# One fused fp32 network on one core: who takes the closing product, when the first weight pieces are split, and where the windowed attention's output is rounded

## The reference, cut to what matters

```python
for layer in range(DEPTH):                       # DEPTH = 2
    h = rms_norm(x, mix_pre_g[layer])
    m = pool_mixer(h, ...) if layer == 0 else swa_sink_attention(q, kk, vv, sinks) @ w_o
    x = x + rms_norm(m, mix_post_g[layer])
    f = conv_glu_ffn(rms_norm(x, ffn_pre_g[layer]), ...)   # 1024 -> 2 x 2816 -> 1024
    x = x + rms_norm(f, ffn_post_g[layer])
```

## Time and profile before

| | |
|---|---|
| median of 3 runs | 1634.32 us (1633.74 to 1635.6) |
| the profiled execution | 1632.63 us, span 1630.9 us |
| TensorE (PE) busy | 1588.7 us, 97% of the span |
| VectorE (DVE) busy | 1015.9 us, 62% |
| ScalarE (ACT) busy | 706.1 us, 43% |
| GpSimd (POOL) busy | 172.3 us, 11% |
| mean granted TensorE clock | 0.991 |

### The profile page before, as it was taken

The page is one execution under the profiler, slowest core; times in us unless marked ns, Lnnn a source line. Parts: engine busy times, 40 slices in busy tenths (PEclk is TensorE's granted clock), DMA queues, the critical chain, the costliest instruction groups (busy, mean ns, idle before and its releaser), DMA issues.

```text
span 1630.9 us, 21359 instructions
## 1 busy us (share of the span) xinstructions
PE 1588.7 (97%) x8046; PEld 1289.0 (79%) x8046; DVE 1015.9 (62%) x1894; ACT 706.1 (43%) x1391; POOL 172.3 (11%) x148
## 2 busy tenths in 40 slices
PE   7999999999998999999999999999999999999997
PEld 6888888888875788888888887766665888888887
DVE  6876666545768577666663376666666555554367
ACT  6544444333457545444442343344444443443252
POOL 0121111000002202111110000000011001110000
PEclk9999999999999999999999999999999999999998
DMA  6133333333120213333322424211110222222231
GB/s 223 55 108 96 97 99 101 105 110 104 46 75 27 75 52 102 96 92 99 102 97 96 139 97 119 64 47 46 40 39 27 97 91 97 97 98 97 97 110 65
DMA packets 91151, 143.69 MB, mean 88 GB/s; under 512 B 8740, under 2 KB 30756, under 8 KB 90920
## 3 DMA queue, kind: packets, MB, share of 16 engines
q1 hardware_dynamic: 88560, 136.58, 26.9%
q10 hardware_dynamic: 2488, 5.75, 1.1%
HBM read 140.19 MB, written 2.10 MB: 87 GB/s over the span
## 4 chain that ended last, share of the span: by engine, by line
PE 93%; DVE 2%; issue 2%; ACT 1%; DMA 1%; SPq 0%; POOL 0%; DVEq 0%; POOLq 0%; ACTq 0%
PE ps L433 23%; PE ps L434 23%; PE ps L435 23%; PE ps L1918 2%; PE ps L1920 2%; PE ps L1919 2%; PE ps L474 2%; PE ps L475 2%; PE ps L476 2%; PE ps L1599 1%; PE ps L1622 1%; PE ps L1642 1%; PE ps L1293 1%; PE ps L1322 1%; PE ps L1242 1%
## 5 line engine op out<-in xcount | busy, mean ns | idle before, releaser
L418 DVE TENSOR_TENSOR wl<-raw,wh 128x512 fp32r<-128x512 f32 (+2 forms) x425 | 307.4, 727 | 406.0 <-ACT wh L409 405.7
L409 ACT ACTIVATE wh<-raw 128x512 fp32r<-128x512 f32 (+2 forms) x425 | 264.6, 627 | 544.3 <-PE ps L435 541.3
L433 PE MATMUL ps<-Hh,wh 128*128 128x512 f32 x1148 | 452.4, 394 | 1.9 <-DVE Hl L1486 1.9
L435 PE MATMUL ps<-Hh,wl 128*128 128x512 f32 x1148 | 448.3, 390 | 0.0
L434 PE MATMUL ps<-Hl,wh 128*128 128x512 f32 x1148 | 448.2, 390 | 0.0
L433 PEld LDWEIGHTS ps<-Hh,wh 128*128 128x128 f32 x1148 | 216.1, 188 | 49.8 <-issue 2.4
L435 PEld LDWEIGHTS ps<-Hh,wl 128*128 128x128 f32 x1148 | 216.1, 188 | 45.8
L434 PEld LDWEIGHTS ps<-Hl,wh 128*128 128x128 f32 x1148 | 216.2, 188 | 44.9 <-issue 0.7
L433 PE MATMUL ps<-AH,wh 128*128 128x512 f32 x416 | 161.8, 389 | 0.0
L434 PE MATMUL ps<-AL,wh 128*128 128x512 f32 x416 | 161.8, 389 | 0.0
L435 PE MATMUL ps<-AH,wl 128*128 128x512 f32 x416 | 161.8, 389 | 0.0
(11 more groups left out here) (334 smaller groups left out, 2171.1 us busy)
## 6 DMA issues: line engine op xcount, KB each, us to landing
raw<-in_w_in SPq DMA_DIRECT2D x216, 256.0 KB, 2.7
raw<-in_w_out SPq DMA_DIRECT2D x104, 256.0 KB, 2.6
raw<-in_w_up SPq DMA_DIRECT2D x64, 256.0 KB, 2.6
raw<-in_w_down SPq DMA_DIRECT2D x32, 256.0 KB, 2.5
raw<-in_w_q SPq DMA_DIRECT2D x16, 256.0 KB, 2.7
raw<-in_w_o SPq DMA_DIRECT2D x16, 256.0 KB, 2.5
raw<-in_w_pg SPq DMA_DIRECT2D x16, 256.0 KB, 2.5
X<-in_xT SPq DMA_DIRECT2D x8, 256.0 KB, 4.6
```

The costliest lines, as they stand in the source:

```text
L409: e.activation(split_in[n][0][:, 0:width], raws[n % NRAW][:, 0:width], ACT.Copy, scale=1.0 if gain is None else gain).then_inc(s_hi, 1)
L418: e.tensor_tensor(wl[:, 0:width], raw, wh[:, 0:width].bitcast(F32), ALU.subtract).then_inc(s_lo, 1)
L433: e.matmul(b, wh[:, o:o + w], xh, start=k == 0, stop=False, skip_group_check=joined)
L435: m = e.matmul(b, wl[:, o:o + w], xh, start=False, stop=k == (nk - 4 if closing else nk - 1), skip_group_check=joined)
```

## The change

- **Takes.** At all four borders the second halves of the four closing tiles are taken from PSUM to `M` by ScalarE (`act_take`), tiles 0 to 2 right behind their squares and tile 3 behind the first `rhs_high`. The first half stays with VectorE. The next group's first product waits for ScalarE's fourth take.
- **First root sooner.** `half_spread(0)` stands at the closing product's third tile of the second half instead of its fourth, VectorE makes the first `scale_m` and `add_m_dve` inside `dve_close`, and `rhs_low(0, 0)` comes first in `dve_new_rhs`. `half_spread(1)` goes from behind two tiles of the first k to behind all of them.
- **First splits spread.** At border 0 the low parts of pieces 7 to 9, all made before the first root was used, and those of 10 and 11 are made one by one behind k = 0 to 4; piece 6 follows the first `add_m_dve`; ScalarE's high parts of 8 and 9 move between the first `rhs_high`.
- **Attention output from PSUM.** ScalarE rounds bank 7 directly into `Hh`, VectorE subtracts from bank 7 into `Hl` at the end of its beat, 16 times each with 128 x 256. The `fill` steps and `wq`'s copy are gone. The next unit's product with the values waits for VectorE's `Hl` (`s_hl`) instead of ScalarE's copy.
- **Sinks.** GpSimd writes them, the first four ahead and each other one ahead of its masks.
- **Planner.** `AHEAD` gets a border for `o`, from the second piece of `q` on. By the lists it gives, two pieces are split at each of steps 1 to 7 of `q0`, and none at `q1` 6 and 7 and at `o0` 0 to 4 (one at each before).

```diff
         def pe_close(e, q, name, xh, xl, nk):
...
-                        if k == 1 and half and i == 3:
+                        if k == 1 and half and i == 2:
                             half_spread(e, q, 0)
...
+                    if half and i < 3:
+                        act_take(e, q, i)
...
+        def act_take(e, q, i):
+
+            e.activation(M[:, 4 + i, 256:512], Q_BANKS[q][i][:, 256:512], ACT.Copy,
+                         scale=post_gain(q, 4 + i)).then_inc(s_pea, 1)
...
             half_variance(e, q, 0)
-            for i in range(2):
-                half_take(e, q, i, 1)
-                add_square(e, q, i, 1)
+            add_square(e, q, 0, 1)
             half_diagonal(e, q, 0)
+            add_square(e, q, 1, 1)
+            scale_m(e, q, 0, 0)
+            add_m_dve(e, q, 0, 0)
             add_square(e, q, 2, 1)
-            half_take(e, q, 2, 1)
...
             if k == 0:
-                scale_m(e, q, 0, 0)
-                add_m_dve(e, q, 0, 0)
-                half_take(e, q, 3, 1)
+                rhs_low(e, j, 0, 0)
                 half_variance(e, q, 1)
                 scale_m(e, q, 1, 0)
-                rhs_low(e, j, 0, 0)
                 add_m_dve(e, q, 1, 0)
...
+        FIRST_LOWS = {4: (7,), 5: (8,), 6: (9,), 7: (10,), 8: (11,)}
...
                 if u > 0:
-                    e.wait_ge(s_wob, u)
+                    e.wait_ge(s_hl, unit_at(u - 1))
...
                 e.wait_ge(s_wav, u + 1)
-                e.activation(wq[:, 2 * p:2 * p + 2, n * P:(n + 1) * P],
-                             banks[7][:, 0:256].rearrange("p (c t) -> p c t", c=2), ACT.Copy).then_inc(s_wob, 1)
+                if n == 0:
+                    e.wait_ge(*used[first["q"] + 8 + 2 * p + 1])
+                e.activation(Hh[:, 2 * p:2 * p + 2, n * P:(n + 1) * P],
+                             banks[7][:, 0:256].rearrange("p (c t) -> p c t", c=2), ACT.Copy).then_inc(s_hh, 1)
...
+            u = b - 3
+            if 0 <= u < 16:
+                p, t = u // 4, slice(u % 4 * P, u % 4 * P + P)
+                e.wait_ge(s_hh, unit_at(u))
+                e.tensor_tensor(Hl[:, 2 * p:2 * p + 2, t], banks[7][:, 0:256].rearrange("p (c t) -> p c t", c=2),
+                                Hh[:, 2 * p:2 * p + 2, t].bitcast(F32), ALU.subtract).then_inc(s_hl, 1)
```

More of the change, by code:

```diff
@@ L336, in pairs_at @@
             return 2 * q
-        AHEAD = ((first["in0"], 0), (first["kv"], first["out0"] + FT + 8), (first["in1"], first["o"] + 8),
-                 (first["z"], first["out1"] + FT + 8))
+        AHEAD = ((first["in0"], 0), (first["kv"], first["out0"] + FT + 8), (first["o"], first["q"] + 1),
+                 (first["in1"], first["o"] + 8), (first["z"], first["out1"] + FT + 8))
         due, split_in, had_by, more_free = {}, {}, {}, {}
@@ L367, in build @@
                     split_in[m] = more[border][at_ - NSPL]
-                    if border > 0 and (before is None or before < AHEAD[border][1]):
-                        more_free[m] = ((s_hl, rhs_at(3, 7)) if border == 2 else
-                                        used[AHEAD[border][1] - 8 + 2 * (at_ - NSPL) + 1])
+                    if border > 0 and border != 3 and (before is None or before < AHEAD[border][1]):
+                        more_free[m] = used[first["kv"] - 1 if border == 2 else
+                                            AHEAD[border][1] - 8 + 2 * (at_ - NSPL) + 1]
                         before = None
@@ L375, in build @@
                     had_by[m] = before
-                held = [new for new, grow in AHEAD if new - 3 <= m < new]
+                held = [new for new, grow in AHEAD if new - 3 <= m < new and new != first["o"]]
                 free_at[at_] = (held[0] if held else m + 1, m)
@@ L606, in act_rhs @@
                             rhs_high(e, j, c, half)
+                            if half == 0 and c == 0:
+                                act_take(e, j, 3)
+                            if j == 0 and half == 0 and c < 2:
+                                split_high(e, 8 + c)
                     rhs_square(e, j, 0)
@@ L639, in pe_first_group @@
                         o += w
-                        if k == 0 and half == 0 and o == 2 * P:
+                        if k == 0 and half == 0 and b is outs[-1]:
                             half_spread(e, j, 1)
@@ L865, in act_pool_mixer @@
                                  scale=col("pool_scale", 4 + i)).then_inc(s_psq, 1)
+                if half:
+                    for i in range(3):
+                        act_take(e, 0, i)
                 if half == 0:
@@ L895, in dve_pool_mixer @@
             e.wait_ge(s_ident, 16)
-            for half in range(2):
-                for i in range(4 - half):
-                    if i < 2:
-                        add_square(e, 0, i, half)
-                    half_take(e, 0, i, half)
-                    if half and i == 1:
-                        half_diagonal(e, 0, 0)
-                if half == 0:
-                    for n in range(4, 7):
-                        split_low(e, n)
-                    half_variance(e, 0, 0)
-            for n in range(7, 10):
-                split_low(e, n)
+            for i in range(4):
+                if i < 2:
+                    add_square(e, 0, i, 0)
+                half_take(e, 0, i)
+            split_low(e, 4)
+            split_low(e, 5)
+            half_variance(e, 0, 0)
+            add_square(e, 0, 0, 1)
+            add_square(e, 0, 1, 1)
+            half_diagonal(e, 0, 0)
+            scale_m(e, 0, 0, 0)
+            add_m_dve(e, 0, 0, 0)
+            split_low(e, 6)
             e.wait_ge(s_cols, 16)
@@ L1117, in dve_ffn @@
                         variance(e, PRE_CHAIN[j], J_BANKS[j][STAT_BANK])
[L1118 removed]
+                    if n0 + 8 * g + k in FIRST_LOWS:
+                        for n in FIRST_LOWS[n0 + 8 * g + k]:
+                            split_low(e, n)
+                    else:
+                        low_ahead(e, n0 + 8 * g + k)
                     if l < 2 and g == 1 and k == 0:
@@ L1400, in pe_window @@
                 if what == "kv" and i[0] == 0:
-                    pe_first_group(e, 1, "kv", 8, [banks[n][:, :] for n in range(4)], (s_pev, taken_at(1, 7)))
+                    pe_first_group(e, 1, "kv", 8, [banks[n][:, :] for n in range(4)], half_taken(1))
                 elif what == "turn":
@@ L1447, in act_window @@
                         act_close(e, 2, "o")
-                elif what == "fill":
-                    k = i[0]
-                    e.wait_ge(*used[first["q"] + 8 + k])
-                    e.wait_ge(s_wob, 4 * (k // 2) + 4)
-                    e.activation(Hh[:, k, :], wq[:, k, :], ACT.Copy).then_inc(s_hh, 1)
                 elif what == "tcopy":
@@ L1482, in dve_window @@
                         dve_close(e, 2)
-                elif what == "fill":
-                    k = i[0]
-                    e.wait_ge(s_hh, rhs_at(3, k))
-                    e.tensor_tensor(Hl[:, k, :], wq[:, k, :], Hh[:, k, :].bitcast(F32), ALU.subtract).then_inc(s_hl, 1)
                 elif what == "turn":
@@ L1497, in dve_window, with set_sinks @@
                     dve_beat(e, i[0])
+        def set_sinks(e, u):
+            if u >= NW:
+                e.wait_ge(s_wex, u - NW + 1)
+            o = COLS["sinks"][0] + u // 4 * 4
+            e.tensor_copy(wSb[u % NW][:, :, P], cols[:, o:o + 4]).then_inc(s_wsk, 1)
         def gpsimd_window(e):
@@ L1502, in gpsimd_window @@
             root(e, PRE_CHAIN[1])
+            for u in range(NW):
+                set_sinks(e, u)
             for u in range(16):
+                if u + NW < 16:
+                    set_sinks(e, u + NW)
                 if u % 4:
```

61 lines of the change are left out of this document (30 added, 31 removed).

## The result

The changed kernel takes 1630.24 us (median of 16 runs, 1627.83 to 1632.83), the kernel before 1635.3 beside it (16 runs, 1633.42 to 1639.61). The ratio is 0.9969, 95% interval 0.9961 to 0.9976: faster by 5.1 us (3.9 to 6.4). The profiled execution took 1630.3 us (span 1628.6), 2.3 less than that of before.

What follows compares the result with a forecast made beforehand. TensorE, busy 97% of the span, bounds the kernel, so only its waits and the clock lost behind them count. Waits 2.6 plus clock 1.9 make 4.5 us, from 1634.32 to 1629.8 us, range 1627.0 to 1633.5.

Steps and rivals of the forecast that it cites:

- Border 1, 0.6: `out0` to `kv`: root spread sooner and ScalarE's takes bring the first product 0.66 sooner; counted 0.6 (0.3 to 0.66).
- Borders 2 and 3, 0 each in waits: First product gains 0.6, but TensorE waits that at k = 3 for `Hl` instead; counted 0 each (0 to 0.6).
- Border 2's clock, 1.2: With 0.6 less idle time in one piece, no fall to 0.50 behind border 2; saves 1.2 us (0 to 1.2).
- Border 0, 0.7: Pool mixer to `in0`: first product 2.1 sooner, mostly given back by k = 6; worth 0.7 (0 to 2.1).
- VectorE needed 20.0 us ... 21.4: Border 0, first scale to `Hl` of k = 6: 20.0 us before, 21.4 after with three more splits, one half take less.
- matters little: Border 0: the half clock at 38.4 matters little, since VectorE and not TensorE sets the time at k = 6.
- Window, 1.3 in waits: Window attention: 1.0 ahead of `o0` 6, 0.4 at GpSimd's masks, minus 0.1 at the two turns; together 1.3.
- The wait for the last `Hl`: End of window attention, ahead of `o0` 6: wait falls from 1.93 to 0.95, saving 1.0 (0.8 to 1.1).
- The clock behind the last `fill`, 0.7: Window attention: the half clock at 553.8 costs 1.7 at most; somewhat under half saved, 0.7 (0 to 1.6).
- the clock falls elsewhere: Rival: waits shrink, but a fall behind border 2 or last `fill` moves behind another wait; only 2.6 us, 1631.7; chance 0.17.
- VectorE takes it back: Rival: borders 0 and 1 give nothing, subtractions ahead of the turns cost 0.6 more; 2.6 us, 1631.7; chance 0.10.
- a loop through bank 7: Rival, window attention: values wait for two engines in series, 0.55 later each of 15 times, 8.3 us; 1638.1; chance 0.05.

Runs made afterwards that it cites:

- window_only: Attention output from PSUM, sinks on GpSimd and the planner's border for `o` alone, with the four borders of the kernel before; 1630.89 us, ratio 0.997.
- late_first: Changed kernel, with TensorE also waiting for the second tile's X before its first product at borders 2 and 3; 1631.58 us, ratio 0.9967.
- turns_late: The edit of late_first on the changed kernel with `turned 3` put ahead of beat 7 and `turned 4` ahead of beat 9; 1624.99 us, ratio 0.9938.

## Why the prediction was right, step by step

- **Border 1, 0.6**: 0.76. The order of the steps was as argued; TensorE's wait fell from 0.91 to 0.16. ScalarE's take was priced too low (0.47 instead of 0.39) and hid all the same.
- **Borders 2 and 3, 0 each in waits**: the new wait at k = 3 came as foreseen (0.51 and 0.42). At an unslowed clock it is 30.49 - 30.27 = 0.22 (old border 2 from window_only) and 30.38 - 30.22 = 0.16.
- **Border 2's clock, 1.2**: 31.55 - 30.49 = 1.06. That the fall goes with the wait is shown by late_first and turns_late and by all 14 executions; whether splitting or shortening it did it is open.
- **Border 0, 0.7**: nothing in the pair of profiles. The failing step is "VectorE needed 20.0 us ... 21.4": from the first scale to k = 6's `Hl` it was 55.78 - 33.73 = 22.05, with a pause of 1.06 in it that was 0.86 in before, and the first scale itself came 0.3 later than taken. The half clock that "matters little" sat on the spreads, for which VectorE waits. Still 0 is only this pair: from the first closing means to the group's mean it is 33.64 to 34.91 in the eight executions that have the changed border 0 and ScalarE's takes, and 34.75 to 35.78 in the three with the old one. The term is inside that, clock included. Where the half clock is equally long, 10.2 us, the second group starts 36.58 behind the first means in window_only (old border) and 35.89 in turns_late (changed border), 0.7 sooner as forecast; with 6.8 us in one piece it is 35.56 and 35.89 against 35.80. So the term depends on where the half clock lies.
- **Window, 1.3 in waits**: 1.4 by the view (1.9 to 0.9, 2.4 to 1.9; in before, line 1322 waited 2.4 in the stage), 1.7 by the stage's length at equal falls. The wait for the last `Hl` was put at 0.95 and is 0.94. `turned 3` stayed at 2.41, since the new subtraction hid in time that VectorE lost anyway: the two additions behind it took 1.82 instead of 2.16 and still ended 0.54 behind the mask. By the Trainium skill, page "SBUF — State Buffer", section "Who interferes with whom", a VectorE instruction with at most one SBUF input does not meet GpSimd's lock; the trace agrees: 12 of the 16 new subtractions run beside a mask, and all 16 take 0.41 to 0.43.
- **The clock behind the last `fill`, 0.7**: no fall there, but one behind `turned 3`, where before had none in its profile. In this pair that term is 0. Over the 14 executions a fall stands at the wait ahead of `o0` 6 in two of the three that wait 1.93 and in one of the eleven that wait 0.94; behind `turned 3`'s 2.4 it came in six of nine.
- **Not foreseen**: the mixer's fall is 6.8 instead of 3.4 and takes 341.21 - 339.62 = 1.6 back. It was 6.8 in all eight kernels with split waits, and in two of the six others. Why is open, but it need not be a price of the falls that went: the length goes with the place of the fall against TensorE's wait of 3.1 us there. Where the fall starts between 1.1 us ahead of the end of that wait and 1.0 behind it, it is 6.8 long (ten of ten); where it starts 1.5 to 2.1 behind, 3.4 (four of four).

The terms of the two profiles are, from the table, -0.76, -1.71, -1.28, -0.16 and +1.59, which is the 2.3 between the spans. The median of all runs gained 5.1. The other 2.8 are executions of before that its one profile does not stand for: it was at 1632.63 and a clock of 0.991, under every one of its 16 runs, and four of those lie above 1639, where the runs with a clock on record have 0.986 or 0.987. So the split of the forecast, 2.6 from waits and 1.9 from the clock, is near what the runs show (some 3 and some 2), but the places of the clock's part were not as argued: it came mostly with the window's part. That the pair of profiles shows half the forecast and the medians more than it is the luck of single executions, and so is part of how close 1629.8 came: the median of before was taken as 1634.32 from three runs and is 1635.3 in sixteen. The rival "the clock falls elsewhere" was thus half true in the profile and not in the median; "VectorE takes it back" held at border 0 alone, in this pair; a loop through bank 7 was not seen.

## What to carry to other kernels

Read the long waits that a change leaves alone: moving two steps ahead of a beat in a written order gave 7 us more, where the whole change, aimed at waits under 2 us, had given 5. No run touched the two longest, 6.9 at the start and 3.1 at the mixer. When an engine works in a written order, a result that another engine needs next belongs ahead of the work that can follow, and its price is the wait plus the clock that falls behind it. A wait in one piece can cost more than its length: of the borders 2 and 3, with 0.97 in one piece, the one that a fall followed cost 1.1 to 1.3 us more, and with 0.3 and 0.5 neither did. And compare runs at the same granted clock: a pair of profiles, or two medians, holds what the clock did in those executions.

## What the runs showed of the hardware

- A fall of TensorE's granted clock to 0.50 lasted 3.4 us or twice that, at border 0 also three times (10.2), and 7.8 to 11.2 at the end of the kernel. It cost 1.1 to 1.6 us for each 3.4 at borders 2 and 3, in the window and at the head of the mixer. It can cost nothing: the mixer is 341.32 and 341.25 in late_first and turns_late, which have no fall near 1231, and 340.94 to 341.34 in the others with 6.8 at its head, which do. The two wait 1.16 and 1.15 longer for ScalarE in its place.
- With the long wait at both borders 2 and 3 the fall followed one of them and never both or neither (six of six). The Trainium skill, "TensorE: Matmul & The Clock Gate", Part 1, has the window free-running, which fits a fall that changes place; that it was always one is told only by these runs.
- A count of removed falls does not give their gain: in every kernel that had none at the borders 2 and 3 the mixer's was 6.8 us instead of 3.4. That one brings the other is not shown.
- GpSimd's sinks of 128 x 4 took 0.19 in the median and 0.66 at most, and no engine waited for one.

```profile
L1528 POOL COPY wSb<-cols x16: 185/189/660, 429.7 to 530.8; 128x4 f32<-128x4 f32 x16
```
